# A hybrid attention decoder on one core: two pieces of the first attention's vector work go to GpSimd, and one rounding to an earlier stage

## The reference, cut to what matters

```python
s_c = einsum('bgrtd,bgnd->bgrtn', qb, kc) * scale          # compressed: 15 blocks of keys
p_c = masked_softmax(s_c, cmp_end[None, :] <= t[:, None])
o_c = einsum('bgrtn,bgnd->bgrtd', p_c, vc)
...
s_s = einsum('bgrtd,bgtkd->bgrtk', qbr, k_sel) * scale     # selected
s_w = einsum('bgrtd,bgkd->bgrtk', qbr, kwb) * scale        # window
...
o = gb[..., 0:1] * o_c + gb[..., 1:2] * o_s + gb[..., 2:3] * o_w
return out @ w_out                                          # the output projection, w_out_a
```

## Time and profile before

| what | value |
|---|---|
| median of 3 runs | 1342.18 us (1341.36 to 1342.96) |
| the profiled execution: its own time | 1342.56 us |
| its span in the profile | 1340.8 us |
| TensorE busy | 1309.3 us, 98% of the span |
| VectorE busy | 396.7 us, 30% |
| ScalarE busy | 281.1 us, 21% |
| GpSimd busy | 73.7 us, 6% |

### The profile page before, as it was taken

The page is one execution under the profiler, slowest core; times in us unless marked ns, Lnnn a source line. Parts: engine busy times, 40 slices in busy tenths (PEclk is TensorE's granted clock), DMA queues, the critical chain, the costliest instruction groups (busy, mean ns, idle before and its releaser), DMA issues.

```text
span 1340.8 us, 31617 instructions
## 1 busy us (share of the span) xinstructions
PE 1309.3 (98%) x14080; PEld 792.6 (59%) x14080; DVE 396.7 (30%) x680; ACT 281.1 (21%) x510; POOL 73.7 (6%) x104
## 2 busy tenths in 40 slices
PE   8998999999999999999999999999999999999996
PEld 6765788888776544644744654564464474465444
DVE  6569576664576411001101101101100010120222
ACT  5465455544455200000010010000000001000001
POOL 2033300000012200000000000000000000000100
PEclk9999999999999999999999999999999999999998
DMA  9681268955542999999999999999999999999992
GB/s 321 197 220 64 86 196 292 360 182 202 147 153 66 381 397 420 417 395 420 418 395 419 419 406 390 420 418 393 420 417 372 419 418 396 407 419 418 418 420 104
DMA packets 115774, 443.16 MB, mean 331 GB/s; under 512 B 11936, under 2 KB 49088, under 8 KB 101312
## 3 DMA queue, kind: packets, MB, share of 16 engines
q1 hardware_dynamic: 108704, 423.39, 81.4%
q10 hardware_dynamic: 5792, 13.63, 2.8%
q0 software_dynamic: 1152, 4.19, 0.8%
HBM read 425.85 MB, written 15.34 MB: 329 GB/s over the span
## 4 chain that ended last, share of the span: by engine, by line
PE 94%; DVE 3%; ACT 2%; issue 1%; DMA 0%; DVEq 0%; ACTq 0%
PE bank L1677 43%; PE bank L1670 22%; PE bank L1537 6%; PE bank L1139 5%; PE bank L1141 5%; PE bank L1140 4%; PE bank L1539 3%; PE bank L1156 2%; PE bank L1413 1%; PE bank L1374 1%; ACT arena L945 1%; PE bank L1282 1%; PE bank L1169 1%; ACT wh L767 0%; PE bank L1462 0%
## 5 line engine op out<-in xcount | busy, mean ns | idle before, releaser
L1677 PE MATMUL bank<-ring,arena 128*32 128x448 f32 x2880 | 275.6, 539 | 0.7 <-issue 0.7
L2168 DVE TENSOR_TENSOR arena<-arena,bank 128x448 f32<-128x448 f32 x48 | 26.9, 616 | 728.0 <-PE bank L1677 728.0
L1677 PEld LDWEIGHTS bank<-ring,arena 128*32 128x32 f32 x2880 | 111.3, 110 | 156.8 <-issue 155.9
L1718 DVE TENSOR_TENSOR wl<-ring,wh 128x2048 fp32r<-128x2048 f32 (+1 forms) x55 | 124.1, 2259 | 57.6 <-ACT wh L767 57.3
L1670 PE MATMUL bank<-ring,arena 128*32 128x256 f32 x2304 | 126.0, 379 | 0.0
L1537 PE MATMUL bank<-hT,wh 128*128 128x512 f32 x344 | 121.6, 399 | 0.0
L767 ACT ACTIVATE wh<-ring 128x2048 fp32r<-128x2048 f32 (+1 forms) x56 | 105.5, 1888 | 34.9 <-PE bank L1141 32.3
L1677 PE MATMUL bank<-whs,arena 128*32 128x448 f32 x1152 | 111.6, 539 | 0.0
L1677 PE MATMUL bank<-wls,arena 128*32 128x448 f32 x1152 | 111.6, 539 | 0.0
L1670 PEld LDWEIGHTS bank<-ring,arena 128*32 128x32 f32 x2304 | 88.3, 110 | 38.6 <-issue 3.6
L1085 ACT ACTIVATE arena<-bank 128x448 f32<-128x448 f32 x48 | 22.6, 544 | 389.6 <-PE bank L1677 389.6
(11 more groups left out here) (287 smaller groups left out, 1304.0 us busy)
## 6 DMA issues: line engine op xcount, KB each, us to landing
ring<-in_moe_w_in_dram SPq DMA_DIRECT2D x120, 896.0 KB
ring<-in_moe_w_out_dram SPq DMA_DIRECT2D x48, 1024.0 KB
whs<-in_moe_w_in_dram SPq DMA_DIRECT2D x48, 896.0 KB, 17.8
wls<-in_moe_w_in_dram SPq DMA_DIRECT2D x48, 896.0 KB, 18.2
arena<-in_moe_w_in_dram SPq DMA_DIRECT2D x32, 896.0 KB, 15.7
whs<-in_moe_w_out_dram SPq DMA_DIRECT2D x24, 1024.0 KB, 21.4
wls<-in_moe_w_out_dram SPq DMA_DIRECT2D x24, 1024.0 KB, 22.3
ring<-in_dense_w_in_dram SPq DMA_DIRECT2D x22, 1024.0 KB
```

The source lines that it names most:

```text
L1677: ins = pe.matmul(bank[s + GROUPS * (kind == "u")][32 * j:32 * j + 32, 0:BLOCK], xgT[:, c, 32 * s:32 * s + 32], slot[:, BLOCK * j:BLOCK * ...
L1718: dve.tensor_tensor(wl[:, n % SPLITS, 0:size], slot_of(n)[:, 0:size], wh[:, n % SPLITS, 0:size].bitcast(F32), ALU.subtract).then_inc(split, 1)
L2168: ins = dve.tensor_tensor(act[:, s, :], act[:, s, :], bank[GROUPS + s][:, 0:BLOCK], ALU.mult)
```

## The change

Three edits in the first attention. GpSimd does the last multiplication of compressed job x (one operation of 128x512 with a broadcast factor in the place of VectorE's L1954), and VectorE signals `weighed` after the gate product instead. GpSimd makes the low part of output item 2 (128x2048, two inputs in SBUF) right behind that in its queue; at stage 18 VectorE waits for the new semaphore `low_made` and counts `split` up by one. ScalarE rounds item 2 at stage 9, ahead of the exponentials of job 9, and no longer at stage 16.

```diff
 def by_pool(job):
 
-    return job[0] == "main" and job[3] == 1
+    return job[3] == 1 if job[0] == "main" else job[3] == 0
...
-ROUND_A, SPLIT_A = (16, len(JOBS_A) + 1), (18, len(JOBS_A) + 2)
+ROUND_A, SPLIT_A = (9, len(JOBS_A) + 1), (18, len(JOBS_A) + 2)
+LOW_AT = 9
...
                     if by_pool(job):
                         w = job[6]
                         pool.wait_ge(weighed, before + pooled(jobs, i + 1))
-                        for k in range(512 // w):
-                            e = ex[i % (LAG + 1)][:, k * w:k * w + w]
-                            ins = pool.tensor_scalar(e, e, rg[:, i % 8, k:k + 1], None, ALU.mult)
+                        if job[0] == "cmp":
+                            e = ex[i % (LAG + 1)].rearrange("p (k n) -> p k n", n=w)
+                            ins = pool.tensor_tensor(e, e, sumc[:, job[3], :].rearrange("p (k n) -> p k n", n=1)
+                                                     .to_broadcast([P, 512 // w, w]), ALU.mult)
+                        else:
+                            for k in range(512 // w):
+                                e = ex[i % (LAG + 1)][:, k * w:k * w + w]
+                                ins = pool.tensor_scalar(e, e, rg[:, i % 8, k:k + 1], None, ALU.mult)
                         ins.then_inc(normed, 1)
+                    if jobs is JOBS_A and i == LOW_AT:
+                        n = AT["out_a"] + 1
+                        pool.wait_ge(rounded, halved(n))
+                        pool.tensor_tensor(wl[:, n % SPLITS, :], slot_of(n), wh[:, n % SPLITS, :].bitcast(F32), ALU.subtract)\
+                            .then_inc(low_made, 1)
...
-                    if i in at:
+                    if not swa and i == at[0]:
+                        dve.wait_ge(low_made, 1)
+                        dve.sem_inc(split, 1)
+                        n_split[0] = n_out + 2
+                    elif i in at:
                         split_weights(n_out + (1 if swa else 2) + at.index(i))
...
-                            step(dve.tensor_tensor(weights, weights,
-                                                   gates[:, tt, 0:16].rearrange("p (a b r) -> p a r b", a=2, b=2), ALU.mult))
-                            dve.tensor_tensor(e, e, sumc[:, tt, :].rearrange("p (k n) -> p k n", n=1).to_broadcast([P, 16, w]),
-                                              ALU.mult).then_inc(normed_v, 1)
+                            ins = dve.tensor_tensor(weights, weights,
+                                                    gates[:, tt, 0:16].rearrange("p (a b r) -> p a r b", a=2, b=2), ALU.mult)
+                            if by_pool(jobs[i - 1]):
+                                ins.then_inc(weighed, 1)
+                            else:
+                                step(ins)
+                                dve.tensor_tensor(e, e, sumc[:, tt, :].rearrange("p (k n) -> p k n", n=1)
+                                                  .to_broadcast([P, 16, w]), ALU.mult).then_inc(normed_v, 1)
```

More of the change, by code:

```diff
@@ L345, in decoder_kernel @@
         normed_v = sem("normed_v")
+        low_made = sem("low_made")
         late_done = sem("late_done")
```

## The result

| what | before | changed |
|---|---|---|
| median of 20 runs | 1342.66 us (1341.36 to 1343.22) | 1344.47 us (1342.70 to 1345.39) |
| the profiled execution: its own time | 1342.56 us | 1344.84 us |
| span | 1340.8 us | 1343.1 us |

The ratio is 1.0015, with a 95% interval of 1.0009 to 1.0021: +2.0 us (+1.2 to +2.8). The change costs about 0.15%, within the 0.2% that the prediction called even.

What follows compares the result with a forecast made beforehand. TensorE was taken as busy nearly all the time, so only its waits, mainly for VectorE's moves, could change the time. -5.1 + 4.3 + 2.1 = +1.3 us on the median 1342.18 gave 1343.5 us, range 1337 to 1346.

Steps and rivals of the forecast that it cites:

- the change without cost: First attention: VectorE 3.5 us earlier, TensorE's waits shrink and its clock stays up; 5.1 us won, between 3.5 and 5.8.
- the hold: Around stages 9 and 10: GpSimd's low part, reading SBUF, keeps a two-input VectorE instruction waiting, 4.3 us lost.
- the clock behind the pause: After TensorE's 4.3 us pause, up to job 14's scores: the clock falls, 3.1 us of work doubles, 2.1 us lost.
- The move behind job x's gate product: VectorE near 104 us: the move can start about 0.08 us behind the product's start, 0.7 us earlier than before.
- The old waits: TensorE at 127.14 and 129.54 us: the 1.27 us wait goes, the 1.77 us one shrinks to about 0.7.
- The row that was to show it: VectorE's multiplication of job 9 was to take some 4.9 us in the place of 0.69.
- The bounds in that paragraph: VectorE's wait for GpSimd's low part: nothing to 4.6 us; 4.1 to 4.6 if held to the operation's end.
- rival 1: VectorE held off and the time even, 1343.5 us likeliest, range 1340.5 to 1345; chance 0.52.
- the slack: VectorE's maximum of job 14 at 114.30 us can take 1.0 us of the clock's loss.
- Rival 2: GpSimd's reads don't hold VectorE: 1337.1 us, or 1338 to 1339 with holds in pieces; chance 0.24.
- Rival 3: The clock falls again at stages 20 to 22, its 2.7 us are not won: +4.0, 1346.2 us; chance 0.19.
- Rival 4: The saved VectorE slots were not on the path: nothing won, 4.3 us lost, 1346.5 us; chance 0.05.

Runs made afterwards that it cites:

- e4_warm: Changed kernel plus 16 bf16 matmuls on unused data in TensorE's pause, to hold the clock up; 1343.52 us, ratio to before 1.0 to 1.0018.
- e1_tiny_low: Changed kernel with GpSimd making only 8 of the 2048 columns of item 2's low part, the rest left out; 1338.08 us, ratio 0.996 to 0.9983.
- e3_low_on_vector: Changed kernel with item 2's low part back on VectorE at stage 18, job x's multiplication still on GpSimd; 1340.54 us, ratio 0.9981 to 0.9999.

## Why the prediction was right, and where it was off

The forecast was +1.3 us and 1343.5; the timed difference is +2.0 us (+1.2 to +2.8), at 1344.47 us. The sum, term by term:

| term | predicted, us | measured, us | from |
|---|---|---|---|
| the change without cost | -5.1 | -4.57 | 37.51 - 42.08 |
| the hold | +4.3 | +4.15 | e4_warm - e1_tiny_low |
| the clock behind the pause | +2.1 | +1.48 | changed - e4_warm |
| sum | +1.3 | +1.06 | 43.14 - 42.08 |

Each measured term is the difference of two single profiled executions, and together they add up to the last row by their making. That the sum came so close is in part luck: the gain was over-rated by 0.5 us and the clock's loss by 0.6, and the two errors cancel.

**The gain.** The move behind job x's gate product starts 0.09 us behind it, as foreseen. ScalarE's rounding costs nothing: it runs from 101.53 to 103.45, and the exponentials of job 9 still wait 0.78 us for their maximum until 104.23. The old waits shrink and the clock stays up at stages 20 to 22. The whole came to 4.57 in the place of 5.1 us. Both of its parts were over-rated a little. In the stretch TensorE is busy 37.18 us before and 34.79 in e1_tiny_low: 2.4 us from the clock, where the prediction had 2.7. It stands idle 4.90 us before and 2.72 in e1_tiny_low: 2.2 us of waits, where the prediction had 2.4 (0.7 + 1.3 + 1.1 - 0.7). The old wait shrank to 0.66 us as foreseen; the new one behind it is 1.22 us.

**The hold.** Mechanism and size were right: one short instruction with two SBUF inputs stands still to the end of GpSimd's low part. The row that was to show it was the wrong one. The prediction let the gate product of job 9 slip through with 0.07 us to spare and had the multiplication behind it caught, with 4.9 us. The product was caught: GpSimd began with job x's multiplication 0.26 us behind the gate product's start, and this took 1.05 us and not 1.26, so the low part began 0.2 us ahead of the gate product. A race with 0.07 us between the two was not to be called from these rows. It changed nothing in the sum, since either instruction is released at GpSimd's end. The bounds in that paragraph were not well added: GpSimd's end at 109.9 to 110.4 less the 105.53 of L1972 gives 4.3 to 4.9 us and not 4.1 to 4.6, and the lower end of rival 1 is 1342.18 - 2.4 = 1339.8 and not 1340.5. The copy's pace of reading was of no use as a bound either: at that pace 2048 numbers are read in 1.7 us, and the one-input kernel held VectorE for 3.65.

GpSimd's 128x2048 operation took 4.52 us, within the 4.5 to 5.05 of the prediction and by the lower of its two readings. The Trainium skill, "GPSIMD Engine Reference", section "Elementwise — side-by-side cycle accounting", gives 4497 ns for an addition of that size; the trace agrees, with 4.50 and 4.52 us for the subtraction.

**The clock.** It fell behind the pause and did not fall a second time. The loss was 1.48 us and not 2.1. The same matmuls, from the transpose behind the pause to the end of the next score pair, take 5.76 us in the changed kernel (114.72 to 120.48) and 3.19 us in e4_warm (113.77 to 116.96). So TensorE loses 2.57 us; the prediction had the work right (3.1 us) and doubled it, which gave a loss of 3.1. Of these 2.57 us, 1.48 reach the end of the stretch, so the slack was 1.1 us, close to the 1.0 of the prediction.

**The rivals.** Rival 2, that GpSimd's reads don't hold VectorE, is refuted by the 4.32 us row; its time, 1337.1, was about right for a kernel without the hold (1338.08). Rival 3, two falls of the clock, didn't come: 1.00 in 128 to 136 us. Rival 4 is refuted by e1_tiny_low and e3_low_on_vector: the saved slots are on the path.

**What the prediction did not see** is that the kernel before has no single length of this stretch. The +1.06 us hold against its first profile; against its third it is 43.14 - 40.98 = +2.16 us. The timed +2.0 lies between the two, near the second. The runs of before fall into a group at about 1341.5 us and one at about 1342.8, and those of the changed kernel into 1343.4 and 1345.2. Three things that can part such groups are in the profiles: the clock at the start of the program (about 1.3 us), the clock behind the old waits (1.1 to 1.35 us), and the clock ahead of the experts (1.2 us, seen in e4_warm alone). Both profiles of the changed kernel, 1344.84 and 1345.29 us, are of its upper group and have the fall at the start, which is ahead of all that the change touches; without it the first would be at about 1343.6, in the lower group. That is an estimate; no execution of the lower group was profiled. How often each fall comes, and whether they come together, was not measured; so how the 0.9 us between +1.06 and +2.0 divide between them, and how much of the timed difference is the change's own, stays open.

## What to carry to other kernels

Before work goes to an idle GpSimd, look at what VectorE does at that time: a long GpSimd operation that reads SBUF stops the next VectorE instruction with two SBUF inputs, however small, and everything behind it (4.3 us here, for 2.2 us of VectorE's work saved). Ask first whether the work can stand elsewhere on the same engine: the low part cost nothing on VectorE eight stages later, ahead of a wait, and that version is 3.8 us faster than before by its ratio where the change is 2.0 us slower. If it has to be GpSimd, cut it in pieces; and if two instructions meet within 0.1 us in a forecast, work out both orders.

## What the runs showed of the hardware

- A hold by GpSimd's reads depends on the operation: to the end for two inputs (4.32 us of 4.52, the product having come 0.22 us late), 3.65 of 5.36 us for one input of 2048, at most 0.5 us for each 256-column piece, and none at all for a memset.
- Eight pieces of 256 columns take 6.42 us on GpSimd where one operation of 2048 takes 4.52. A piece takes 0.73 us at the median, eight of them 5.8; the longest takes 1.18, and what is above 5.8 us fits GpSimd being held by VectorE's two-input instructions in its turn.
- GpSimd's multiplication of 128x512 with a broadcast factor takes 1.05 us, less than the 1.262 us of its operation on two plain inputs of that size.
- After the same two waits, to 0.01 us, TensorE's clock fell in all three executions of the kernel before, and in one it was back sooner, which shortened the stretch by 1.1 to 1.35 us; one profile is not enough to price such a stretch.
